# When SyncE announces expert weights, and where the residual rows are loaded, in a mixture-of-experts stage

## The chip, the cores and the metric

The kernel runs on one core of a Trainium2 chip. A core has engines that work side by side: TensorE (PE in the profile), VectorE (DVE), ScalarE (ACT), GpSimd (POOL) and SyncE (SP), which here only waits, counts and issues transfers. Sixteen DMA engines move data between HBM and the on-chip memory SBUF. The metric is the time of one launch on the device, in microseconds (us), as the median of several runs.

## The reference

One step of a hybrid decoder layer: modulated layer norm, a mixer (RG-LRU and Mamba-2 SSD), a residual with layer norm, then a hierarchical mixture of experts and a last residual with layer norm. The change is in the last two. Cut to what matters:

```python
def hmoe(v, ...):                      # v: 1032 rows (1024 prompt, 8 sample) of 1024
    # each row goes to 2 of 32 experts; rows are grouped by expert, 32 experts in all
    hb = jax.nn.silu(xb @ w_gate[e]) * (xb @ w_up[e])     # w_gate, w_up: 1024 x 512
    return hb @ w_down[e]                                  # w_down: 512 x 1024

f = hmoe(concat(vp, vs))
xp = layer_norm(alpha * xp + mp[:, 5] * f[:n_p], ln2_g, ln2_b)
xs = layer_norm(alpha * xs + ms[:, 5] * f[n_p:], ln2_g, ln2_b)
```

All is float32, so an expert has 2.1 MB each of gate, up and down weights, 6.3 MB together, and all 32 experts are read: 201 MB.

## The kernel before, in words

The first 900 us or so (mixer, first residual, routing) are not touched. The residual rows xp that the last layer norm needs are written to HBM (`xp1_d`) by then.

*Blocks.* The rows are sorted by expert and cut into blocks; this input gives 82. A block takes, on TensorE in this order: a turn of the previous block's hidden values (`h_turn`, line 2209), its own gate/up product (`gate_up`, line 2200, 64 matmuls), the turn of the input rows of the block after (`x_turn`, line 2188), and the down product of the previous block (`down`, line 2218, 32 matmuls). So the down product of block k comes behind the gate/up product of block k+1.

*Order of experts.* After three fixed ones the experts come in trios: a big one (3 to 9 blocks) and two small ones (1 or 2 blocks). Here x counts experts in this order, 0 to 31. The big ones are 3, 6, ... 27, growing; the small ones from expert 16 on have one block each. "Trio end" is the place where experts 1 or 2 after a big one and the next big one begin in three blocks in a row (19, 20, 21; 22, 23, 24; 25, 26, 27; 28, 29, 30).

*Weights.* They live in one large tile, `ring`. TensorE reads only the working copy `wcur`. Three slots (`GU_AT`) hold gate and up weights that have been fetched ahead, two (`DN_AT`) hold down weights. When a block belongs to a new expert, ScalarE copies the gate weights from slot to `wcur` (line 2000, four pieces of about 1 us) and VectorE the up weights (line 2579, four pieces of 0.7 us), each piece as soon as TensorE has used the matching quarter of the old ones (`gu_mm`). VectorE then copies the down weights (line 2592, one operation of 2.3 to 2.5 us) after the previous block's down product. On VectorE these stand between `h_out` of one block (lines 2541 and 2545, which makes the down product's input) and that of the next. On ScalarE the gate copy stands in front of `hb_out` (line 1972), which TensorE's next `h_turn` waits for.

*Announcements.* The copies don't wait for the loads themselves. SP waits for a load and then adds one to `gu_here` (gate and up) or `dn_here` (down); the copying engines wait for these counts:

```python
act.wait_ge(gu_here, here)
for q in range(QW):
    act.wait_ge(gu_mm, before * QW + (q + 1))
    act.activation(wcur[:, 1024 * q:1024 * q + 1024], ring[:, bass.ds(w + 1024 * q, 1024)], ...)
```

*SP's loop over experts.* SP does everything in one order. In iteration x it: waits for gate/up x and counts `gu_here`; waits until the down weights of x-1 have been copied and issues the load of down x+1 (line 1689); waits for down x and counts `dn_here`; waits until gate and up of x have been copied and issues the two loads of gate/up x+3 (line 1683). Where many transfers are queued an issue itself can take 4 to 6 us of SP's time. Behind the gate/up load in iteration 0 stand two tiles of residual rows (`xf[0]`, `xf[1]`, which have room of their own). In iteration 29 (`NE - 3`), where no gate/up load is left to do, stand six more tiles, the row `gate2` and the tile of eight sample rows; they go into gate/up slot `GU_AT[1]`. A tile is 128 rows of 1024, 0.52 MB.

*Other queues.* GpSimd gathers the input rows of each block (line 1833) and scatters its output rows (line 1841) by indirect DMA.

*The finale.* After the last scatter SP loads the result rows of each tile (`load_f`, line 1745, two loads of 0.52 MB per tile, four tiles ahead) into slot `GU_AT[2]`. For tile 0 ScalarE (line 2040) and VectorE (2641) combine them; for the others TensorE does (2254). VectorE then adds the residual tile `xf[t]` (2652) and does the layer norm's passes (2661, 2667). VectorE waits once for `gate2`, `ln2g`, `ln2b`.

Of the kernel before, what the change touches and what calls it, by code (L numbers as in the profile page):

```python
# [29 lines left out]
P = 128  # L30
D = 1024
KT = D // P
SEQ = 1024
NT = SEQ // P
DEC = 8
# [8 lines left out]
NE = 32  # L44
# [36 lines left out]
def build_step(nc, x_prompt, x_sample, c_prompt, c_sample, state_lru_conv, state_lru_h, state_ssd_conv,  # L81
# [13 lines left out]
    with ctx:  # L95
# [1531 lines left out]
        with nc.Block() as block:  # L1627
            @block.sync
            def _(sp):
# [72 lines left out]
                for x in (1, 2):  # L1702
                    load_gate_up(x, expert_at(x))
                    load_down(x, expert_at(x))
                for x in range(NE):
                    sp.wait_ge(gu_loaded[(x - 1) % 3 if x else 3], 32 * ((x + 2) // 3 if x else 1))
                    sp.sem_inc(gu_here, 1)  # L1707
                    if x >= 2 and x + 1 < NE:
                        e = expert_at(x + 1)
                        sp.wait_ge(down_copied, copied_down(x - 1))  # L1710
                        load_down(x + 1, e)
                    sp.wait_ge(dn_loaded[(x - 1) % 2 if x else 2], 16 * ((x + 1) // 2 if x else 1))
                    sp.sem_inc(dn_here, 1)
                    if x == 0:
                        sp.wait_ge(vector_once, IDXS_READY)
                        sp.wait_ge(tensor_once, TOKS_MM)
                        for b, n in ((0, 5), (1, 4)):
                            sp.wait_ge(xp1_stored[b], 16 * n)
                        load_gate_up(3, expert_at(3))
                        for t in range(2):  # L1720
                            sp.dma_start(xf[t], xp1_d[t * P:(t + 1) * P, :]).then_inc(xf_loaded[t], 16)
                    if x >= 1 and x + 3 < NE:
# [4 lines left out]
                        load_gate_up(x + 3, e)  # L1727
                    if x == NE - 3:
                        chunks = copied_gate_up(x)
                        sp.wait_ge(gate_copied, chunks)  # L1730
                        sp.wait_ge(up_copied, chunks)
                        for t in range(2, NT):
                            sp.dma_start(xf[t], xp1_d[t * P:(t + 1) * P, :]).then_inc(xf_loaded[t], 16)
                        sp.dma_start(gate2, mod_d[0:1, 5 * D:6 * D].to_broadcast([P, D])).then_inc(rows2n_loaded, 16)
                        sp.dma_start(xf[NT][0:DEC, :], xp1_d[SEQ:SEQ + DEC, :]).then_inc(xf_loaded[NT], 16)
                sp.wait_ge(down_copied, copied_down(NE - 2))
# [974 lines left out]
```

## Time and profile before

| | us |
|---|---|
| median of 3 runs | 1550.19 (1548.47 to 1551.68) |
| the profiled execution | 1546.65 |
| its span, first to last instruction | 1545.0 |
| TensorE busy | 1368.3 (89% of the span) |
| VectorE busy | 955.2 (62%) |
| ScalarE busy | 571.5 (37%) |
| first gate/up product of the expert stage | starts at 910.2 |
| last down product | starts at 1479.3 |

The profile is of one execution; times in it count from the span's start. The expert stage is some 570 us of it, the finale 63. A row of the timeline gives start and duration in us, engine, line, operation, and in brackets how long the engine stood idle before it and what ended that. "SPq" is SyncE's own instruction queue. DMA shares are of sixteen engines; 1.03 is what the rows show when they are all full.

### The profile page before, as it was taken

Reading aid. Unit: us, or ns where it says so; the run is one execution under the profiler, and the core shown is the slowest. Engines: PE = TensorE matmul, PEld = TensorE weight load, DVE = VectorE, ACT = ScalarE, POOL = GpSimd, SP = SyncE. Lnnn points to the kernel's source line nnn. Section 1 sums busy time; section 2 is a strip of 40 time slices with the busy share of each in tenths; the row PEclk is TensorE's granted clock in tenths of the full one; section 3 lists DMA queues with packets and bytes.
Section 4 is the critical chain, followed back from the end, with each engine's and each line's share of the span. In section 5 each row is a group of like instructions: output and inputs, shape, how many; then the busy total and the mean of one; then the engine's idle time right before and its main releaser. Section 6 shows DMA issues by size and latency. Waiting matters only on the chain.

```text
span 1545.0 us, 38250 instructions
## 1 busy us (share of the span) xinstructions
PE 1368.3 (89%) x13487; PEld 1010.1 (65%) x13487; DVE 955.2 (62%) x1702; ACT 571.5 (37%) x886; POOL 298.8 (19%) x325
## 2 busy tenths in 40 slices
PE   4799999999999998799999269899898999999864
PEld 3688989999888887687688145445454544545431
DVE  6655553968998889785775655444444244251549
ACT  3322322525556566621222014343334234141533
POOL 4000002210000000200000024333343333333320
PEclk9899999999999999899999579999999999999987
DMA  9666415644343345722225949999999897977763
GB/s 284 197 233 243 141 41 173 202 153 125 111 125 111 123 140 200 278 96 83 87 83 185 400 163 406 407 406 407 407 406 393 341 405 298 370 273 283 301 240 152
DMA packets 169586, 365.87 MB, mean 237 GB/s; under 512 B 16040, under 2 KB 94944, under 8 KB 166312
## 3 DMA queue, kind: packets, MB, share of 16 engines
q1 hardware_dynamic: 150616, 308.72, 54.5%
q0 software_dynamic: 18320, 54.08, 10.0%
q10 hardware_dynamic: 576, 2.10, 0.4%
q8 instruction: 45, 0.74, 0.2%
q14 instruction: 29, 0.24, 0.0%
HBM read 324.06 MB, written 45.63 MB: 239 GB/s over the span
## 4 chain that ended last, share of the span: by engine, by line
PE 38%; DVE 8%; DMA 5%; SPq 3%; issue 3%; ACT 1%; ACTq 1%; DVEq 0%; POOLq 0%
PE PS L2200 15%; PE PS L2069 10%; PE PS L2218 7%; DMA ring<-in_w_down_dram 5%; SPq L1683 2%; PE PS L2188 2%; PE PS L2209 2%; DVE ring L2592 1%; DVE big L2270 1%; PE PS L2100 1%; PE PS L2135 1%; DVE ring L2647 1%; PE PS L2092 1%; DVE ring L2652 1%; DVE ring L2661 1%
## 5 line engine op out<-in xcount | busy, mean ns | idle before, releaser
L939 PE MATMUL PS<-big 128*128 128x344 f32 x2592 | 426.0, 325 | 1.7 <-DVE big L1192 1.7
L939 PEld LDWEIGHTS PS<-big 128*128 128x128 f32 x2592 | 414.9, 191 | 10.4 <-issue 6.7
L2200 PE MATMUL PS<-ring,arena 128*32 128x256 f32 x5248 | 314.5, 394 | 0.5 <-DVE arena L2537 0.5
L2200 PEld LDWEIGHTS PS<-ring,arena 128*32 128x32 f32 x5248 | 167.5, 114 | 123.1 <-issue 29.8
L1833 POOL DMA_INDIRECT arena<-v_d,icur x84 | 103.4, 1231 | 315.0 <-DVE icur L2549 216.5
L2218 PE MATMUL PS<-ring,arena 128*32 128x256 f32 x2624 | 158.6, 382 | 1.0 <-DVE arena L2545 1.0
L2000 ACT ACTIVATE ring<-ring 128x1024 f32 x124 | 121.0, 1046 | 103.7 <-SPq L1707 84.1
L1841 POOL DMA_INDIRECT f_d<-arena,scur x82 | 107.9, 1316 | 55.6 <-issue 49.0
L2537 DVE COPY arena<-PS 128x256 f32<-128x256 f32 x82 | 34.7, 424 | 129.4 <-PE PS L2188 129.4
L2218 PEld LDWEIGHTS PS<-ring,arena 128*32 128x32 f32 x2624 | 77.1, 110 | 53.2 <-DVE arena L2545 1.3
L2541 DVE SCALAR_TENSOR_TENSOR arena<-arena,PS 128x128 f32<-128x128 f32 x82 | 23.6, 288 | 136.0 <-ACT arena L1977 99.8
L2579 DVE COPY ring<-ring 128x1024 f32 x124 | 80.3, 689 | 32.7 <-SPq L1707 26.1
L1972 ACT ACTIVATE arena<-PS 128x256 f32<-128x256 f32 x82 | 30.7, 374 | 179.7 <-PE PS L2200 179.7
L2069 PE MATMUL PS<-low 128*128 128x512 f32 x256 | 83.2, 407 | 11.0 <-ACTq L1913 5.1
L2592 DVE COPY ring<-ring 128x4096 f32 x31 | 74.7, 2409 | 28.9 <-PE PS L2218 28.9
L2069 PE MATMUL PS<-big,low 128*128 128x512 f32 x256 | 80.6, 397 | 0.0
L2069 PE MATMUL PS<-low,big 128*128 128x512 f32 x256 | 80.1, 395 | 0.0
L1982 ACT ACTIVATE arena<-PS 128x256 f32<-128x256 f32 x82 | 31.3, 382 | 116.1 <-PE PS L2218 116.1
L2209 PE MATMUL PS<-ident,arena 128*128 128x128 f32 x164 | 37.7, 314 | 40.3 <-ACT arena L1972 40.3
L2209 PEld LDWEIGHTS PS<-ident,arena 128*128 128x128 f32 x164 | 17.1, 146 | 74.4 <-ACT arena L1972 44.8
L2069 PEld LDWEIGHTS PS<-low 128*128 128x128 f32 x256 | 47.1, 193 | 21.8 <-issue 8.2
L1154 DVE TENSOR_TENSOR big<-arena,big 128x1024 fp32r<-128x1024 f32 x20 | 24.5, 1225 | 56.7 <-ACT big L713 56.6
(469 smaller groups left out, 1875.2 us busy)
## 6 DMA issues: line engine op xcount, KB each, us to landing
ring<-in_w_gate_dram SPq DMA_DIRECT2D x32, 2048.0 KB, 12.8
ring<-in_w_up_dram SPq DMA_DIRECT2D x32, 2048.0 KB, 18.7
ring<-in_w_down_dram SPq DMA_DIRECT2D x32, 2048.0 KB, 23.6
arena<-in_w_ada_dram SPq DMA_DIRECT2D x16, 1024.0 KB, 6.7
arena<-in_w_in_dram SPq DMA_DIRECT2D x20, 512.0 KB, 8.0
upper<-in_w_ada_dram SPq DMA_DIRECT2D x8, 1024.0 KB, 11.6
upper<-in_w_in_dram SPq DMA_DIRECT2D x16, 512.0 KB, 4.0
arena<-acs_d SPq DMA_DIRECT2D x8, 1024.0 KB, 4.7
```

Source lines behind the costliest of these rows:

```text
L939: mm = pe.matmul(PS[:, 3 * b + a, 0:CU], wss[b][:, i, k, :], us[:, j, k, a * CU:(a + 1) * CU], start=(k == 0 and (i, j) == PARTS[0]), stop ...
L1833: gp.indirect_dma_start(xg[b], None, v_q, bass.IndirectOffsetOnAxis(ap=icur[b][:, :], axis=0), bounds_check=QW * (SEQ + DEC) - 1, oob_is_e ...
L1841: gp.indirect_dma_start(f_q, bass.IndirectOffsetOnAxis(ap=scur[b][:, :], axis=0), yo[b], None, bounds_check=QW * 2 * (SEQ + DEC) - 1, oob_ ...
L1982: act.activation(yo[b], PS[:, 6, 0:DQ], ACT.Copy).then_inc(yo_ready, 1)
L2000: act.activation(wcur[:, 1024 * q:1024 * q + 1024], ring[:, bass.ds(w + 1024 * q, 1024)], ACT.Copy).then_inc(gate_copied, 1)
L2069: mm = pe.matmul(PS[:, bank + n, :], (yh[h % 2], yl3[h % 3])[a][:, k, :], (WH, WL)[b][i][:, 512 * n:512 * n + 512], start=(k == 0 and (a, ...
L2200: mm = pe.matmul(PS[32 * g:32 * g + 32, 3, 0:FH], xT[:, c, CAP * q:CAP * q + CAP], wcur[:, w:w + FH], start=(q == 0 and c == 0), stop=(q = ...
L2209: mm = pe.transpose(PS[:, 4, P * c:P * c + P], hb[:, P * c:P * c + P], ident[:, :])
L2218: mm = pe.matmul(PS[32 * g:32 * g + 32, 6, 0:DQ], hT[:, c % 2, CAP * (c // 2):CAP * (c // 2) + CAP], wcur[:, 8192 + 1024 * c + DQ * g:8192 ...
L2537: ve.tensor_copy(xT, PS[:, 0, 0:2 * P].rearrange("p (c t) -> p c t", c=2)).then_inc(xT_ready, 1)
L2579: ve.tensor_copy(wcur[:, 4096 + 1024 * q:5120 + 1024 * q], ring[:, bass.ds(w + (4096 + 1024 * q), 1024)]).then_inc(up_copied, 1)
L2592: ve.tensor_copy(wcur[:, GU:GU + DN], ring[:, bass.ds(w, DN)]).then_inc(down_copied, 1)
```

## The change

SP waits for gate/up x+1 and counts `gu_here` at the start of iteration x, where it did so at the start of iteration x+1; the count for expert 0 is made before the loop. The wait for down x and its count now stand before the load of down x+1. The two residual tiles of iteration 0 and the loads of iteration 29 are issued after the loop, behind all weights, together.

```diff
--- before.py
+++ after.py
@@ -1702,37 +1702,37 @@
                 for x in (1, 2):
                     load_gate_up(x, expert_at(x))
                     load_down(x, expert_at(x))
+                sp.wait_ge(gu_loaded[3], 32)
+                sp.sem_inc(gu_here, 1)
                 for x in range(NE):
-                    sp.wait_ge(gu_loaded[(x - 1) % 3 if x else 3], 32 * ((x + 2) // 3 if x else 1))
-                    sp.sem_inc(gu_here, 1)
+                    if x + 1 < NE:
+                        sp.wait_ge(gu_loaded[x % 3], 32 * ((x + 3) // 3))
+                        sp.sem_inc(gu_here, 1)
+                    sp.wait_ge(dn_loaded[(x - 1) % 2 if x else 2], 16 * ((x + 1) // 2 if x else 1))
+                    sp.sem_inc(dn_here, 1)
                     if x >= 2 and x + 1 < NE:
                         e = expert_at(x + 1)
                         sp.wait_ge(down_copied, copied_down(x - 1))
                         load_down(x + 1, e)
-                    sp.wait_ge(dn_loaded[(x - 1) % 2 if x else 2], 16 * ((x + 1) // 2 if x else 1))
-                    sp.sem_inc(dn_here, 1)
                     if x == 0:
                         sp.wait_ge(vector_once, IDXS_READY)
                         sp.wait_ge(tensor_once, TOKS_MM)
                         for b, n in ((0, 5), (1, 4)):
                             sp.wait_ge(xp1_stored[b], 16 * n)
                         load_gate_up(3, expert_at(3))
-                        for t in range(2):
-                            sp.dma_start(xf[t], xp1_d[t * P:(t + 1) * P, :]).then_inc(xf_loaded[t], 16)
                     if x >= 1 and x + 3 < NE:
                         e = expert_at(x + 3)
                         chunks = copied_gate_up(x)
                         sp.wait_ge(gate_copied, chunks)
                         sp.wait_ge(up_copied, chunks)
                         load_gate_up(x + 3, e)
-                    if x == NE - 3:
-                        chunks = copied_gate_up(x)
-                        sp.wait_ge(gate_copied, chunks)
-                        sp.wait_ge(up_copied, chunks)
-                        for t in range(2, NT):
-                            sp.dma_start(xf[t], xp1_d[t * P:(t + 1) * P, :]).then_inc(xf_loaded[t], 16)
-                        sp.dma_start(gate2, mod_d[0:1, 5 * D:6 * D].to_broadcast([P, D])).then_inc(rows2n_loaded, 16)
-                        sp.dma_start(xf[NT][0:DEC, :], xp1_d[SEQ:SEQ + DEC, :]).then_inc(xf_loaded[NT], 16)
+                chunks = copied_gate_up(NE - 3)
+                sp.wait_ge(gate_copied, chunks)
+                sp.wait_ge(up_copied, chunks)
+                for t in range(NT):
+                    sp.dma_start(xf[t], xp1_d[t * P:(t + 1) * P, :]).then_inc(xf_loaded[t], 16)
+                sp.dma_start(gate2, mod_d[0:1, 5 * D:6 * D].to_broadcast([P, D])).then_inc(rows2n_loaded, 16)
+                sp.dma_start(xf[NT][0:DEC, :], xp1_d[SEQ:SEQ + DEC, :]).then_inc(xf_loaded[NT], 16)
                 sp.wait_ge(down_copied, copied_down(NE - 2))
                 for dst, src in ((ln2g, ln2_g), (ln2b, ln2_b)):
                     sp.dma_start(dst, src.to_broadcast([P, D])).then_inc(rows2n_loaded, 16)
```

## Rows read from the trace of the kernel before

**Rows 1.** Table of waits, 910 to 1482 us, ScalarE, then TensorE (total, times, longest).

```profile
ACT ring L2000 <- SPq L1707: 84.1, 9, 38.9
...
PE PS L2209 <- ACT arena L1972: 40.3, 10, 7.3
```

**Rows 2.** Stretches: length, busy time and count by engine, TensorE's clock, DMA share, GB/s.

```profile
920.00:1170.00 250.00, 237.50 (x3688) 129.34 (x3684) 112.23 (x254) 89.06 (x166) 92.98 (x73) 0.97 1.03 407
1172.00:1180.00 8.00, 8.00 (x133) 4.34 (x126) 4.42 (x11) 6.56 (x10) 2.15 (x3) 1.00 0.86 331
1420.00:1440.00 20.00, 20.00 (x331) 11.04 (x324) 5.86 (x19) 7.41 (x14) 6.15 (x7) 1.00 0.12 39
```

**Rows 3.** Timeline at expert 27: start, duration, instruction [idle before, what ended it].

```profile
1363.81 3.66 PE L2200 MATMUL PS<-ring,arena 128*32 128x256 f32 x64
...
1370.07 3.66 PE L2200 MATMUL PS<-ring,arena 128*32 128x256 f32 x64
...
1375.65 3.90 ACT L2000 ACTIVATE ring<-ring 128x1024 f32 x4 [4.93 <-SPq L1707]
...
1379.87 0.69 PE L2209 MATMUL PS<-ident,arena 128*128 128x128 f32 x2 [3.83 <-ACT arena L1972]
...
1380.49 4.99 PE L2200 MATMUL PS<-ring,arena 128*32 128x256 f32 x64
```

**Rows 4.** Line 1689: down load of expert 26, ns and start, then landing.

```profile
L1689 SPq DMA_DIRECT2D ring<-in_w_down_dram x1: 4250/4250/4250, 1324.3 to 1324.3; - x1
...
DMA to landing us min/median/max: 25.0/25.0/25.0
```

**Rows 5.** Stretch after the stall of expert 27 (columns of rows 2).

```profile
1380.40:1382.00 1.60, 1.60 (x17) 0.80 (x20) 0.95 (x3) 0.28 (x1) 1.29 (x2) 0.50 1.02 417
```

**Rows 6.** Line 1689: down load of expert 18.

```profile
L1689 SPq DMA_DIRECT2D ring<-in_w_down_dram x1: 373/373/373, 1185.0 to 1185.0; - x1
...
DMA to landing us min/median/max: 13.3/13.3/13.3
```

**Rows 7.** Timeline of TensorE at expert 18.

```profile
1194.29 5.92 PE L2200 MATMUL PS<-ring,arena 128*32 128x256 f32 x64
...
1202.81 3.66 PE L2200 MATMUL PS<-ring,arena 128*32 128x256 f32 x64
...
1206.84 1.93 PE L2218 MATMUL PS<-ring,arena 128*32 128x256 f32 x32
```

**Rows 8.** Timeline of VectorE, ScalarE and TensorE at experts 28 to 30.

```profile
1440.26 0.29 DVE L2541 SCALAR_TENSOR_TENSOR arena<-arena,PS 128x128 f32<-128x128 f32 x1 [2.38 <-issue]
...
1444.42 3.66 PE L2200 MATMUL PS<-ring,arena 128*32 128x256 f32 x64
...
1446.97 0.29 DVE L2541 SCALAR_TENSOR_TENSOR arena<-arena,PS 128x128 f32<-128x128 f32 x1 [0.22 <-issue]
...
1453.49 3.90 ACT L2000 ACTIVATE ring<-ring 128x1024 f32 x4 [8.63 <-SPq L1707]
...
1457.71 0.69 PE L2209 MATMUL PS<-ident,arena 128*128 128x128 f32 x2 [7.33 <-ACT arena L1972]
```

**Rows 9.** Line 1689: down loads of experts 30 (lands first) and 31.

```profile
L1689 SPq DMA_DIRECT2D ring<-in_w_down_dram x2: 373/390/408, 1446.9 to 1458.9; - x2
...
DMA to landing us min/median/max: 10.2/11.7/13.3
```

**Rows 10.** Timeline of TensorE: the last two down products.

```profile
1475.99 1.91 PE L2218 MATMUL PS<-ring,arena 128*32 128x256 f32 x32
...
1479.30 1.93 PE L2218 MATMUL PS<-ring,arena 128*32 128x256 f32 x32 [1.03 <-DVE arena L2545]
```

**Rows 11.** Line 1738, issued at 1472.8: landing of two broadcast norm rows.

```profile
DMA to landing us min/median/max: 4.1/4.6/5.1
```

**Rows 12.** Chain that ended last, the finale's start (start, duration, what).

```profile
1484.74 0.33 SPq L1745
...
1485.11 4.53 DMA ring<-f_d
```


## The prediction, made before the changed kernel was run

> **What bounds the kernel now.** I read the waits first, then the stretches, then one stall in the timeline. TensorE is the serial line of the expert stage: 82 blocks, each a gate/up product, a turn and a down product. An undisturbed block takes 6.26 us (1370.07 - 1363.81) [rows 3]. The table of waits shows where it does not run: TensorE stood idle 40.3 us in ten waits for ScalarE's line 1972, and ScalarE stood idle 84.1 us in nine waits for SyncE's line 1707, the count `gu_here` [rows 1]. One of the nine (38.9 us) ends at the start of the stage, so 45.2 us are in eight. The stretches say what else is near: the DMA engines are full from 920 to 1170 us (407 GB/s), and before the last experts nearly idle (share 0.12) [rows 2]. So there are two regimes: up to about expert 18 the weights' traffic is a second limit just behind the queue's announcements, after it TensorE is alone.
>
> One stall, expert 27: TensorE's block begins at 1370.07. ScalarE copies the next expert's gate weights a quarter behind TensorE's quarters, so it could begin 3.66/4 = 0.9 us into the block and a little for the signal, at about 1371.2. It starts at 1375.65, when SP has issued another gate/up pair and only then counts `gu_here` up. ScalarE's `hb_out` is behind the copy, so TensorE's next turn is at 1379.87 after 3.83 us idle, and the block after it lasts 4.99 instead of 3.66 us [rows 3], at a granted clock of 0.50 [rows 5], the lower of the two levels (1.2 of 2.4 GHz), which it got after this idle time. The data was not late: the down load of expert 26 was issued after expert 27's gate/up and landed at 1324.3 + 25.0 = 1349.3 [rows 4]. Price: 1380.49 - 1370.07 - 6.26 = 4.16, plus 4.99 - 3.66 = 1.33, together 5.5 us. Two more trios (experts 21 and 24) have the same stall at 3.8 us idle each; expert 30's is 7.33 us idle, since seven residual loads and a broadcast row are issued in front of its announcement [rows 8].
>
> **Part 1, announcing a step sooner.** In iteration x SP now waits for gate/up x+1 and counts before it waits for anything that compute releases. Expert 27 would be announced before 1349.3, 22 us ahead of need. This adds no instruction; it makes `load_down(x+1)` wait behind two landings, gate/up x+1 and down x. The first of these was queued before down x, so it adds nothing to the second. At the landing of down x the queue still holds gate/up x+2, 4.19 MB or 10.3 us at 407 GB/s [rows 2]. SP answers a landing in 0.7 us (1472.16 to 1472.8), and a 0.52 MB row then lands in 4.1 us of which 1.3 are transfer, so 2.8 us of latency [rows 11]: 3.5 us against 10.3 of cover. Without that cover each expert would cost the difference; that is the slower rival.
>
> What is late next? A stall that goes is replaced by the next limit, the landing of the down weights. From a down landing to the down product takes 1475.99 - 1472.16 = 3.83 us (VectorE's copy 2.3 to 2.5, then `h_out`, which stands behind it on VectorE) [rows 9, 10].
>
> *Experts 1 to 18.* Here several stalls would vanish one after another (about 30 us in blocks 0 to 41 by the same reckoning), but the transfers don't get faster, so I take the last limit. Expert 18's down weights landed at 1185.0 + 13.3 = 1198.3 [rows 6], its down product began at 1206.84 [rows 7]: slack 8.5 - 3.83 = 4.7 us. The full queue itself moves earlier by the two residual tiles that are no longer in it, 1.05 MB / 407 = 2.6 us, and perhaps by the 1.4 us that a dip in it cost (1172 to 1180: share 0.86 where 1.03 is full) [rows 2]. So 7.3 to 8.7 us, I take 8.0. TensorE then waits at that place (the removed stalls exceed the limit) and restarts at the low level: 1.33 us at expert 27, 5.92 - 3.66 = 2.26 at expert 18 [rows 3, 7]; I take 1.6. Term: 6.4, bounds 5.0 (7.3 - 2.3) and 8.7 (no restart).
>
> *Trios 21, 24, 27.* 3 x 5.4 = 16.2 us can go. Is the down load in time? In the last trio, for which the same positions hold, down 30 was issued by an event that doesn't move in its block's frame and landed at 1446.9 + 10.2 = 1457.1 [rows 9]. With no stall the blocks after the one at 1444.42 [rows 8] start at 1450.68 and 1456.94, and the down product 4.03 us later (1206.84 - 1202.81) [rows 7], at 1460.97. Needed: 1457.1 + 3.83 = 1460.9. It fits with nothing to spare. VectorE is the other limit: a round with both copies takes 1446.97 - 1440.26 = 6.71 us [rows 8], 0.45 over TensorE's 6.26; two such rounds put the third `h_out` at 1460.4 and, after its two operations of 0.29, its result at 1461.0, or 1461.4 with copies of 2.5. I take 0.5 us lost per trio, bounds 0 and 0.9. Term: 14.7, bounds 13.5 and 16.2.
>
> **Part 2, residual tiles last.** *Before the finale*, in the frame of the trace: expert 30 isn't held at 1453.5 any more, and down 31 is not behind 3.7 MB. It is issued when down 30 has landed (1457.2; expert 29's copy is done before 1446.97 + 6.71 = 1453.7), alone in the queue: 2.8 + 2.10 MB / 407 = 8.0 us, landed 1465.2, down product of block 80 at 1469.0 (unheld it would be about 1467), last down product 3.3 later (1479.30 - 1475.99 [rows 10]) at 1472.3 instead of 1479.3: 7.0 us earlier, and the first result load could be issued at 1484.74 - 7.0 = 1477.7 [rows 12].
>
> *The finale.* Nine residual tiles, the gate row and two norm rows are 8 x 0.524 + 3 x 0.524 + small = 5.83 MB, 14.3 us. They start at 1465.2 + 0.7 + 2.8 = 1468.7 and end at 1483.0; the result rows `f12` are behind them on SP's queue. Tile 0 (1.05 MB) is there at 1485.6, against 1485.11 + 4.53 = 1489.64 [rows 12]: 4.0 us earlier, not 7.0. SP's issuing (some ten issues of 0.4 us) is hidden in this. Tiles 1 and up come every 2.6 us while VectorE takes 5.2 a tile, so nothing else moves. Term: 4.0. Bounds: 7.0 if these loads overlap freely, 1.3 if the last scatter also has to wait for the queue to drain.
>
> The Trainium skill, page "DMA: Bandwidth & Descriptors", section "Queues, rings and completion order", says that each DMA engine takes turns between the queue rows it has work for, a packet at a time. By it GpSimd's last scatter is slowed but doesn't stand behind SP's loads, which gives the 4.0; strict order would give 1.3. No row here separates the two. The same page, section "Where 436 GB/s comes from", says that about 358 GB/s of HBM bind such loads; the row of 920 to 1170 us shows 407, so the measurement decides. By 358 the finale would be 16.3 instead of 14.3 us and the sum 2 us worse.
>
> **Sum.** 6.4 + 14.7 + 4.0 = 25.1 us, bounds 19.8 and 31.9. The profiled execution took 1546.65 us (span 1545.0 and 1.65 around it), which gives 1521.5; it is 3.5 under the median of the three runs, so for the median of 1550.19 I say 1525.1, bounds 1530.4 and 1518.3.
>
> **Rivals.**
>
> *Down weights take the place of the announcement.* The fit above has no margin: if in three consecutive rounds of copies, gathers and scatters down x lands 2 us later, each of the four last trios keeps 2 us and a restart of 1.6, 14.4 in all: a gain of 10.7, 1539.5 us. For it: the zero margin. Against it: the queue is otherwise idle there [rows 2], and nothing is added to it.
>
> *All of it is real.* No restart at expert 18, no VectorE loss, finale uncontended: 31.9 us, 1518.3. Against it: the finale's bytes are certain.
>
> *No change.* SP's count isn't what holds the copy. Rows 3 and 4 speak against it (data 26 us old when the copy starts). 1550.
>
> *Slower: the queue runs dry.* The change lets fewer transfers stand in the queue at each down landing (4.19 instead of 6.29 MB). If DMA engines ran dry for b us at each of the 15 experts 4 to 18, the cost is 15b; it eats the whole gain at b = 1.7 and at 2.5 gives 1562 us. For it: the dip at 1172 to 1180, while a down load was still pending. Against it: it is one dip of 1.4 us in 250, and 10.3 us of cover against 3.5.
>
> The page's section "Rules for kernel authors" tells to issue a DMA early and wait for it late, and the moved residual tiles do the opposite. As a mechanism here this is the finale's contention. Priced from rows it takes 3.0 of the 7.0 us and can't turn the sign alone: without the gain ahead of it, down 31 (issued at 1458.9 into an empty queue, landed 1466.9) would have its followers through at 1484.7, when the result loads are only issued.
>
> **Chances.** Forecast 0.67; down weights late 0.12; all real 0.08; something larger 0.03; no change 0.04; slower 0.06. The range 1515 to 1539 holds the forecast, the full gain and half of the second. A difference within 0.2% (3 us) is about what a measurement of this kernel can't tell from none. Faster 0.90, same 0.04, slower 0.06.
>
> **What would show it.** Right: ScalarE's copy no longer waits for SyncE's count; TensorE's ten waits shrink to a few at the landings of down weights before expert 19; blocks at 6.26 us through experts 19 to 30; the DMA share stays at 1.03 from 920 on. In the finale one packed stretch of DMA ahead of the result rows, ScalarE waiting for them. Wrong: dips in the DMA share after each down landing, VectorE or SP named at each expert change, or the result rows landing as late as before.

## The result, and the profile after

The changed kernel took 1527.31 us, median of 4 runs (1522.45 to 1529.17), where the kernel before took 1549.34 in the same comparison: ratio 0.9851, 95% interval 0.9825 to 0.9876. The prediction was 1525.1, in the range 1515 to 1539. A second comparison of the same two kernels gave 0.9875 (0.9855 to 0.9895). The profiled execution took 1527.24 us, its span is 1525.3.

The table of waits, 910 to 1482 us, of the kernel after; the rows answer to [rows 1]:

```profile
ACT ring L2000 <- PE PS L2200: 58.0, 30, 36.6
...
DVE ring L2592 <- SPq L1712: 41.3, 10, 7.4
...
PE PS L2218 <- DVE arena L2545: 21.9, 7, 5.0
...
PE PS L2209 <- ACT arena L1972: 1.4, 1, 1.4
...
ACT ring L2000 <- SPq L1710: 0.8, 1, 0.8
```

ScalarE waits for SyncE's `gu_here` once for 0.8 us, where it was 84.1 us in nine waits. Of these 84.1, the 38.9 us at the start of the stage have not gone: the wait there is 36.6 us now and is put down to TensorE (line 2200). What went is the 45.2 us of the other eight. TensorE's waits for `hb_out` fell from 40.3 to 1.4 us. In their place stand waits for the down weights: VectorE 41.3 us for `dn_here` (line 1712), TensorE 21.9 us at down products for `h_out`.

The stretches of the kernel after (columns as in [rows 2]):

```profile
920.00:1170.00 250.00, 237.50 (x3712) 128.43 (x3706) 112.50 (x257) 90.96 (x169) 92.38 (x74) 0.97 1.03 406
1172.00:1180.00 8.00, 8.00 (x132) 4.25 (x124) 5.08 (x14) 5.80 (x10) 2.04 (x2) 1.00 0.96 372
1400.00:1420.00 20.00, 20.00 (x322) 10.86 (x318) 5.86 (x19) 7.26 (x15) 6.17 (x7) 1.00 0.25 97
```

The DMA engines are as full as before up to 1170 us, and the dip at 1172 to 1180 is most of the way closed (share 0.96 for 0.86). Before the last experts they are still mostly idle (0.25 in the third row).

*Where the time went.* The kernel's first part, which the change doesn't touch, ended at 910.23 us in one profile and at 911.81 in the other. So I compare places in the expert stage from each kernel's own first gate/up block, and give each as a difference. A block's excess is its length over the undisturbed 6.26 us.

| us from the stage's first block | before | after | earlier by |
|---|---|---|---|
| down product of expert 18 | 296.61 | 289.80 | 6.8 |
| block 45, after expert 18 | 311.36 | 307.27 | 4.1 |
| block 77, before the last trio end | 527.93 | 507.65 | 20.3 |
| last down product | 569.06 | 543.02 | 26.0 |
| ScalarE begins tile 0 of the result | 579.43 | 558.02 | 21.4 |
| end of the span | 634.80 | 613.53 | 21.3 |

The expert stage alone is 26.0 us shorter and the finale gives 4.8 back. The excess of all blocks fell from 55.2 us in 19 blocks to 25.6 in six; the six are at big experts 6, 9, 12 and 18 (4.3, 6.5, 6.8 + 0.5, 7.0 + 0.8 us). The trio ends of experts 21 to 30, which lost 5.3 us and more each, are free.

The timeline of the kernel after at expert 27, which answers to [rows 3]:

```profile
1358.03 3.90 ACT L2000 ACTIVATE ring<-ring 128x1024 f32 x4 [0.57 <-PE PS L2200]
...
1363.06 3.66 PE L2200 MATMUL PS<-ring,arena 128*32 128x256 f32 x64
...
1369.32 3.66 PE L2200 MATMUL PS<-ring,arena 128*32 128x256 f32 x64
...
1369.81 2.29 DVE L2592 COPY ring<-ring 128x4096 f32 x1 [1.96 <-SPq L1712]
...
1373.41 1.93 PE L2218 MATMUL PS<-ring,arena 128*32 128x256 f32 x32
```

ScalarE's copy is ended by TensorE's quarter, not by SyncE; the blocks follow at 6.26 us. The last two rows are the prediction's narrow fit: VectorE waits 1.96 us for the down weights of expert 27, copies them, and the down product begins 4.09 us behind the gate/up product in front of it, where 4.03 is undisturbed. There was no margin.

At expert 18, answering to [rows 7]:

```profile
1192.51 3.66 PE L2200 MATMUL PS<-ring,arena 128*32 128x256 f32 x64
...
1198.43 2.29 DVE L2592 COPY ring<-ring 128x4096 f32 x1 [7.38 <-SPq L1712]
...
1201.62 3.64 PE L2218 MATMUL PS<-ring,arena 128*32 128x256 f32 x32 [5.01 <-DVE arena L2545]
1205.19 0.69 PE L2209 MATMUL PS<-ident,arena 128*128 128x128 f32 x2
1205.81 4.41 PE L2200 MATMUL PS<-ring,arena 128*32 128x256 f32 x64
```

Here the down weights are the limit: their load is in the chain that ended last, up to its landing at 1198.26.

```profile
1182.56 15.70 DMA ring<-in_w_down_dram
```

TensorE stands 5.01 us and then works at the low level of its clock, as the stretch behind the wait shows (its granted clock is the 0.50):

```profile
1201.60:1204.00 2.40, 2.38 (x24) 1.19 (x28) 0.55 (x3) 0.00 (x0) 0.72 (x1) 0.50 1.03 410
```

The finale of the kernel after, in the chain that ended last (compare [rows 12]):

```profile
1428.24 10.42 DMA ring<-in_w_down_dram
...
1440.00 7.99 DMA ring<-in_w_down_dram
...
1451.50 1.93 PE PS L2218 x32
...
1454.83 1.98 PE PS L2218 x32
...
1458.10 6.29 DMA f_d<-arena,scur
...
1464.45 0.34 SPq L1745
...
1465.78 6.58 DMA ring<-f_d
```

The first two rows are the loads of the down weights of experts 30 and 31. The last scatter took 6.29 us. In the kernel before, where SyncE's norm rows had landed by then [rows 11], the same row of the chain reads:

```profile
1482.56 2.11 DMA f_d<-arena,scur
```

The result rows of this chain, the fourth load of line 1745, took 6.58 us; they are not those of [rows 12] (4.53), which belong to the second load, so these two are not compared. What stood in SyncE's queue meanwhile, by its timeline:

```profile
1448.70 0.82 SPq L1733 DMA_DIRECT2D arena<-xp_d  x2
1449.57 3.14 SPq L1733 DMA_DIRECT2D ring<-xp_d  x6
1452.75 0.50 SPq L1734 DMA_DIRECT2D ring<-mod_d  x1
1453.30 0.38 SPq L1735 DMA_DIRECT2D ring<-xp_d  x1
1454.50 0.36 SPq L1738 DMA_DIRECT2D ring<-in_ln_g_dram  x1
1454.90 1.26 SPq L1738 DMA_DIRECT2D ring<-in_ln_b_dram  x1
```

The two norm rows of line 1738 landed 10.6 and 12.4 us after their issue, the later one at 1467.3.

### The profile page after: what moved, and what is told of

Its sections match the earlier page's. It is cut to its first block, busy times and chain, and to the rows that moved or that the text cites. A ratio compares the mean times of both kernels' runs of the same rounds, so it can differ in the third digit from the quotient of the medians.

```text
span 1525.3 us, 38250 instructions
## 1 busy us (share of the span) xinstructions
PE 1360.6 (89%) x13487; PEld 1005.5 (66%) x13487; DVE 952.6 (62%) x1702; ACT 572.0 (37%) x886; POOL 295.9 (19%) x325
## 3 DMA queue, kind: packets, MB, share of 16 engines
q1 hardware_dynamic: 150616, 308.72, 55.2%
## 4 chain that ended last, share of the span: by engine, by line
PE 29%; DMA 19%; DVE 7%; issue 2%; SPq 1%; ACT 0%; DVEq 0%; POOLq 0%; ACTq 0%
DMA ring<-in_w_down_dram 18%; PE PS L2069 10%; PE PS L2200 8%; PE PS L2218 5%; DVE big L2270 1%; PE PS L2188 1%; PE PS L2100 1%; DMA ring<-in_w_up_dram 1%; PE PS L2135 1%; PE PS L2209 1%; DVE ring L2647 1%; DVE ring L2652 1%; PE PS L2092 1%; DVE ring L2661 1%; SPq L1678 1%
## 5 line engine op out<-in xcount | busy, mean ns | idle before, releaser
L939 PEld LDWEIGHTS PS<-big 128*128 128x128 f32 x2592 | 411.9, 189 | 10.4 <-issue 6.7
L2200 PE MATMUL PS<-ring,arena 128*32 128x256 f32 x5248 | 301.0, 381 | 0.5 <-DVE arena L2537 0.5
L2200 PEld LDWEIGHTS PS<-ring,arena 128*32 128x32 f32 x5248 | 162.1, 110 | 114.2 <-issue 15.0
L2218 PE MATMUL PS<-ring,arena 128*32 128x256 f32 x2624 | 165.1, 394 | 21.9 <-DVE arena L2545 21.9
L2218 PEld LDWEIGHTS PS<-ring,arena 128*32 128x32 f32 x2624 | 78.7, 112 | 78.4 <-DVE arena L2545 23.7
L2592 DVE COPY ring<-ring 128x4096 f32 x31 | 72.7, 2345 | 55.9 <-SPq L1712 41.3
L2069 PEld LDWEIGHTS PS<-low,big 128*128 128x128 f32 x256 | 49.3, 193 | 10.9
L2069 PEld LDWEIGHTS PS<-big,low 128*128 128x128 f32 x256 | 49.2, 192 | 10.8
```

The source lines that it names most:

```text
L939: mm = pe.matmul(PS[:, 3 * b + a, 0:CU], wss[b][:, i, k, :], us[:, j, k, a * CU:(a + 1) * CU], start=(k == 0 and (i, j) == PARTS[0]), stop ...
L2069: mm = pe.matmul(PS[:, bank + n, :], (yh[h % 2], yl3[h % 3])[a][:, k, :], (WH, WL)[b][i][:, 512 * n:512 * n + 512], start=(k == 0 and (a, ...
L2200: mm = pe.matmul(PS[32 * g:32 * g + 32, 3, 0:FH], xT[:, c, CAP * q:CAP * q + CAP], wcur[:, w:w + FH], start=(q == 0 and c == 0), stop=(q = ...
L2218: mm = pe.matmul(PS[32 * g:32 * g + 32, 6, 0:DQ], hT[:, c % 2, CAP * (c // 2):CAP * (c // 2) + CAP], wcur[:, 8192 + 1024 * c + DQ * g:8192 ...
L2592: ve.tensor_copy(wcur[:, GU:GU + DN], ring[:, bass.ds(w, DN)]).then_inc(down_copied, 1)
```

## Experiments

Diffs are against the changed kernel unless said otherwise. Ratios are to the kernel before, with 95% intervals. "In the frame" means counted from the stage's first block, as in the table above.

### The changed kernel again

> The changed kernel once more, to compare the next ones with it on one chip: 1527 us, ratio 0.985 to the kernel before.

1527.34 us, ratio 0.9875 (0.9855 to 0.9895). In the frame every place lies within 0.4 us of the first profile and the end within 0.02 us, so the column "after" does not depend on one execution. The kernel before has one profile only.

### The announcements alone

The residual loads go back to iterations 0 and 29:

```diff
                         load_gate_up(3, expert_at(3))
+                        for t in range(2):
+                            sp.dma_start(xf[t], ...)
...
+                    if x == NE - 3:
+                        (waits for the copies; tiles 2 to 7, gate2, sample rows)
-                (the same behind the loop, with tiles 0 to 7)
```

> Part 1 alone: announcements a step sooner and the down load behind the wait for the down weights, with the residual tiles back in their old places. Theory (announcements remove the stalls, the weights' traffic caps experts 4 to 18, the finale's traffic takes some back): the trios of experts 21, 24, 27 stay free of stalls as in the changed kernel. The two early tiles (1.05 MB, 2.6 us at 407 GB/s) are back in the full queue, so the down product of expert 18 comes 2 to 3 us later than with the whole change. At the end down 31 is again behind 3.7 MB (9 us), so the last down product is about 5 us later than in the changed kernel (1454.8), but the results' loads find an almost empty queue and the scatter takes 2.1 instead of 6.3 us, which gives about the same back. Sum: 2 to 4 us slower than the changed kernel, about 1530 us, 19 us faster than before. Rival (moving the residual tiles is itself the larger part): 1540 or more.

1530.94 us, ratio 0.9883 (0.9868 to 0.9898); in the frame 16.1 us shorter than before. Expert 18's down product is 3.8 us earlier than before (6.8 with both parts). Its down weights land at 289.5 in the frame, which is 1.5 us later than in the kernel before (288.1) and 3.1 later than with both parts (286.4):

```profile
1183.64 16.00 DMA ring<-in_w_down_dram
```

Blocks 45 to 77 take 200.5 us, as with both parts (200.4), where the kernel before took 216.6: the gain at the trio ends is the announcements' alone. What the second part changes is seen in the tail, in the chain that ended last:

```profile
1440.47 14.09 DMA ring<-in_w_down_dram
...
1466.60 2.10 DMA f_d<-arena,scur
```

The last down load, queued behind what is left of 3.7 MB of residual tiles and gate row, takes 14.09 us instead of 7.99, and TensorE's wait at that down product is 8.39 us (3.34 with both parts). The last down product comes 10.2 us later than with both parts, twice the 5 us expected. In exchange the last scatter takes 2.10, and the finale as a whole is 5.1 us shorter, so the sum came out near the forecast all the same.

### The residual tiles alone

The old loop, and all residual loads behind it:

```diff
                 for x in range(NE):
-                    if x + 1 < NE:
-                        (wait for gate/up x+1, count gu_here)
-                    (wait for down x, count dn_here)
+                    (wait for gate/up x, count gu_here)
                     (load_down(x + 1))
+                    (wait for down x, count dn_here)
```

> Part 2 alone: all nine residual tiles behind the last weights, announcements as before. Theory: the stalls at experts 6 to 27 stay as they were (3.8 to 5.3 us idle each); expert 30's shrinks from 7.3 to about 3.8 us idle because nothing is issued in front of its announcement; of these 3.8 us gained some 1 is lost to the finale's traffic. About 3 us faster than before, 1546. Rival (the finale's traffic costs more than that stall, so part 2 alone is slower): 1551 or more.

1543.0 us, ratio 0.9958 (0.994 to 0.9976); 4.8 us shorter in the frame, of which 2.8 are there at block 45. ScalarE still waits for `gu_here` (84.3 us in 11 waits), and TensorE for ScalarE:

```profile
ACT ring L1997 <- SPq L1707: 84.3, 11, 37.7
...
PE PS L2206 <- ACT arena L1969: 36.8, 10, 5.7
```

The excess of blocks 48, 57 and 67 is 4.1 us each as before, that of 78 to 80 together 6.7 for 9.3. The two parts gave 16.1 and 4.8 alone and 21.3 together: they add up to within 0.4 us. The rival "no change" is out, since moving the counts alone took ScalarE's waits and 16.1 us away.

### Half the down weights of experts 5 to 18

```diff
-                    sp.dma_start(ring[:, w:w + DN]..., w_down[0, bass.ds(e, 1)]...)
+                    c = FF // P // 2 if 5 <= x <= 18 else FF // P
+                    sp.dma_start(ring[:, w:w + 1024 * c]..., w_down[0, bass.ds(e, 1), 0:c * P]...)
```

> The changed kernel, but the down loads of experts 5 to 18 bring only half of their rows (1.05 instead of 2.10 MB); the other half of the slot keeps older weights, so this leaves out part of the loading. Theory (the weights' traffic is the limit there): a sixth less traffic is 12.9 us per expert against 14.6 of TensorE work, so the waits at the down products of experts 6, 9, 12 and 18 (together 25 us over undisturbed blocks) go, and the profile's span is 22 to 26 us shorter, about 1500 to 1503, with VectorE's rounds at changes of expert the next limit at 0 to 0.5 us each. Rival (those waits come from SP's order of waiting, or from VectorE's rounds of copies): the waits stay, 1520 or more.

This kernel leaves out half of what these loads bring. One run: 1504.85 us. The sum of the excess is -0.1 us, so no block up to expert 18 is held any more, and block 45 begins 26.0 us sooner than with full loads, as much as their whole excess of 25.6. This shows the limit that is left: at the four big experts among the first 19 the weights arrive too late. The edit removes more traffic (14.7 MB) than the waits needed, so it gives no price per us of transfer.

### The down load in front of the wait for the landing

```diff
-                    sp.wait_ge(dn_loaded[...], ...)
-                    sp.sem_inc(dn_here, 1)
                     if x >= 2 and x + 1 < NE:
                         sp.wait_ge(down_copied, copied_down(x - 1))
                         load_down(x + 1, e)
+                    sp.wait_ge(dn_loaded[...], ...)
+                    sp.sem_inc(dn_here, 1)
```

> The whole change, but load_down(x+1) is issued before the wait for down x again, as in the kernel before. It asks what that move costs. Theory (10 us of cover make it free at experts 4 to 18; it costs only at the end, where down 31 is issued when down 30 has landed, 1440.0, although expert 29's copy was done at 1434.3): the waits at the down products of experts 6, 9, 12, 18 stay within 0.5 us of the changed kernel's (4.3, 6.5, 6.8, 7.8 us over an undisturbed block, restart included); down 31 is issued about 5 us sooner, the 3.3 us wait at the last but one down product goes, the residual tiles are through 4 to 5 us sooner, and the whole is 4 to 6 us faster than the changed kernel, about 1522. Rival (the queue runs short at each down landing in the changed kernel): the early waits shrink by 1 us or more each, and the time is 1517 or less.

1524.58 us, ratio 0.9839 (0.9821 to 0.9857). The intervals overlap with the changed kernel's, so the gain is read in the frame: 2.5 us, where 4 to 6 were expected. The early blocks keep 4.8, 6.5, 6.8 and 6.0 us (sum 25.1 for 25.6), and expert 18's down product is no sooner (290.2 in the frame for 289.8): the queue hadn't run dry behind the landings, so the slower rival has nothing here. Block 42 alone went from 7.0 + 0.8 to 6.0, more than the 0.5 us allowed for. What it does change is the tail. The last down load goes out at 1433.97 instead of 1440.00, its down product is not held any more, and the last one is 4.1 us sooner in the frame; the end is only 2.5 sooner, since the scatter again runs beside the residual loads (the chain of this kernel) and is issued 4.1 us after the last down product, where it was 3.3:

```profile
1454.95 5.91 DMA f_d<-arena,scur
...
1460.92 0.34 SPq L1745
```

### Eight more tiles in the finale

To see how the last scatter and the result rows share the DMA engines with what SyncE has queued, 4.19 MB of further loads are issued behind the residual tiles, into a slot that is free:

```diff
+                (waits for the copies of the last expert)
+                for t in range(NT):
+                    sp.dma_start(ring[:, GU_AT[0] + D * t:GU_AT[0] + D * (t + 1)], xp1_d[t * P:(t + 1) * P, :])...
```

> The changed kernel with eight more loads of residual tiles (4.19 MB, 10.3 us) into a slot that is free, behind the eight real ones: the finale's suspected cost almost doubled. Theory: the first result tile is there 10 us later and the span is 10 us longer, 1535. It also tells how the last scatter shares the DMA engines: if the queues take turns, it lands some 6 us after its issue as in the changed kernel and the result loads are issued at about 1464 to 1466; if it stands behind SyncE's queue, it lands 10 us later and they are issued at about 1475, and the span is 13 us longer. Rival (the finale isn't held by this traffic): span unchanged.

One run: 1532.89 us, 8.4 longer in the frame than the changed kernel, where 10 were expected. Its chain:

```profile
1455.80 5.48 DMA f_d<-arena,scur
1461.30 0.02 SPq L1755
1461.35 0.33 SPq L1751
...
1463.10 15.47 DMA ring<-f_d
```

The scatter, on GpSimd's queue, takes 5.48 us, no longer than with half the bytes ahead of it (6.29). The result rows, on SyncE's own queue, take 15.47 instead of 6.58, 8.9 more, against 10.3 us of added transfer. So a full queue of SyncE's delays this scatter by a few us that did not grow when the queue did, and delays SyncE's own later loads by most of what was added. By the rule of the Trainium skill, page "DMA: Bandwidth & Descriptors", section "Queues, rings and completion order" (the engines take turns between queue rows, a packet at a time), that is what one would see. The two scatters agree with it and rule out a strict order, in which the scatter would have stood behind all eight added tiles, all issued before it, by 1455.0.

### Half of the residual tiles behind the first result rows

On top of the experiment with the down load in front: tiles 4 to 7 and the sample rows are issued behind the result rows of the first four tiles.

```diff
-                for t in range(NT):
+                for t in range(RING):
                     sp.dma_start(xf[t], ...)
...
+                (behind the result rows of the first four tiles)
+                for t in range(RING, NT):
+                    sp.dma_start(xf[t], ...)
```

> As the kernel with the down load issued before the down wait (1524.6), and residual tiles 4 to 8 are loaded behind the first eight result loads instead of in front of them. Theory (what stands in front of the result rows in the full queue, and slows the last scatter, is the finale's price): 9.1 instead of 14.3 us of traffic end at about 1456 in that kernel's frame, the last scatter lands 3 us after its issue instead of 6, the first tile is there 3 us sooner, the time is 1521 to 1522. Rival (the scatter's 6 us are its own, or tiles 4 to 8 come late for VectorE's passes, 5.2 us a tile): no gain, 1524 or more.

1519.91 us, ratio 0.9829 (0.9809 to 0.9849), the shortest time of a kernel that loads everything; 6.1 us shorter in the frame than the changed kernel. The scatter's row in the chain is now

```profile
1454.12 4.10 DMA f_d<-arena,scur
```

and tile 0's first pass begins 12.8 us after the last down product, where it was 15.0 in the changed kernel and 10.4 in the kernel before. The chain shows something that the changed kernel has not, a scatter of an earlier block, issued together with the residual loads:

```profile
1444.64 8.13 DMA f_d<-arena,scur
```

ScalarE waits 1.3 us for its landing before it can write the last block's output, and so the last scatter is issued later. With the down load in front the same wait is 1.8 us. An earlier start of the residual loads moves them onto this scatter.

### Two of the tiles back among the weights

On top of the last: tiles 0 and 1 are issued in iteration 24, where the queue is idle.

```diff
+                    if x == NE - 8:
+                        for t in range(2):
+                            sp.dma_start(xf[t], ...)
```

> As the kernel with the split, and residual tiles 0 and 1, which have room of their own, are loaded in iteration 24, behind gate/up 27, where the DMA engines have idle time (1330 to 1350). Theory: 6.5 us of traffic are left in front of the finale and end before the last scatter is issued; it lands after 2.1 us as in the kernel before, the result loads are issued at once, and the first tile is there 1 to 1.5 us sooner than with the split: 1520. The trio at experts 25 to 27 stays free of stalls. Rival (these loads delay down 26 or 27 and the stall comes back): 1524 or more.

1522.21 us, ratio 0.9837 (0.9816 to 0.9857). The last scatter takes 2.11 us, as alone (the earlier one still 8.12, and ScalarE waits 1.4 us for it), and the frame is 1.0 us shorter than the last one's; the intervals of the two ratios overlap, so the medians don't tell them apart (this execution's untouched first part was 2.9 us longer).

### Gate and up behind the big expert's down load

The limit that is left is the down weights of big experts, which stand in the queue behind gate/up pairs that are needed later. Here the pairs 7, 10, ... 28 are issued behind that down load. The edits from here on are on top of the split of the residual tiles.

```diff
+                HELD = range(4, 26, 3)
...
                         load_down(x + 1, e)
+                    if x - 1 in HELD:
+                        (waits for the copies of x-1)
+                        load_gate_up(x + 2, e)
...
-                    if x >= 1 and x + 3 < NE:
+                    if x >= 1 and x + 3 < NE and x not in HELD:
```

> As the split kernel (1519.9), and the gate/up load that follows the small experts before a big one (gate/up 7, 10, 13, 16, 19, 22, 25, 28) is issued behind the big expert's down load instead of in front of it. The waits that are left (experts 6, 9, 12, 18, 25.6 us in all) end at the landing of a big expert's down weights, behind 4.19 MB that aren't needed for three blocks or more. Theory (limit is the traffic in front of those down weights): they need 10.3 us less in front of them, a saving that counts once over the stage because the traffic itself stays, with one or two restarts less; the waits shrink from 25.6 to some 12 to 15 us and the time to 1507 to 1510. Rival (the queue is too short at the landings now: a down load of 5.2 us of traffic covers SP's 3.5 us, and the DMA engines run dry): the waits stay above 20 us and the time above 1515.

Missed: 1575.04 us, ratio 1.0148 (1.013 to 1.0165), slower than the kernel before. The table of waits of this kernel:

```profile
DVE ring L2601 <- SPq L1723: 67.8, 7, 13.3
...
PE PS L2227 <- DVE arena L2554: 53.2, 7, 11.3
```

and SyncE's own:

```profile
SPq L1711 <- DMA ring<-in_w_up_dram: 193.5, 25, 11.4
```

(84.4 us in 24 waits in the changed kernel.) TensorE's waits at down products grew from 21.9 to 53.2 us: at blocks 42, 50, 59 and 69 the excess is 12 to 13 us each, where the changed kernel lost 7.0 at the first and nothing at the others. SyncE waits in the changed loop for gate/up x+1 before down x. With the pair now issued behind down x, that wait ends last, and the down weights are announced only when the pair behind them has landed. The chain shows it at expert 18, from the pair's load to the count:

```profile
1184.18 17.86 DMA ring<-in_w_up_dram
...
1203.82 0.02 SPq L1723
```

I had moved the transfers and overlooked the announcements. The rival of the expectation, an emptier queue, is there too: the DMA share is 0.20 from 1176 to 1184 us and 0.80 from 1170 to 1200, where the changed kernel has 1.01. What that part costs wasn't separated.

### The same, with the residual loads moved as well

Further: tiles 0 and 1 in iteration 24, and tiles 2, 3 and the gate row issued before the wait for the last down load.

> The same, with residual tiles 0 and 1 in iteration 24, and the residual tiles 2 and 3 with the gate row issued before the wait for down 31 instead of behind it. Theory: what stands in front of the first result rows starts 3.5 us sooner (SP's answer and a transfer's latency) and is 1.05 MB less; it is through before the last scatter is issued, which lands in about 2 us; 2 us faster than the kernel before it, about 1506. Rival (the finale is no longer held by this traffic): equal.

Missed with it: 1571.43 us, ratio 1.0114 (1.0096 to 1.0133). In the frame it ends within 0.2 us of the one before, so the residual loads' place gains nothing here.

### The swap, with the announcement of down x first

In the iterations in which the pair stands behind down x, SyncE now waits for and counts down x before it waits for gate/up x+1:

```diff
-                    if x + 1 < NE:
+                    if x + 1 < NE and x - 2 not in HELD:
                         (wait for gate/up x+1, count gu_here)
...
                     (wait for down x, count dn_here)
+                    if x - 2 in HELD:
+                        (wait for gate/up x+1, count gu_here)
```

> The swap of loads was 25 us slower than before instead of 10 us faster than the split kernel. Its trace shows waits of 12 to 13 us at the down products of experts 18, 21, 24 and 27, ended by SyncE's count for the down weights, while SyncE itself waited for gate/up x+1, which the swap had put behind down x. Here, in the iterations of big experts, SyncE waits for down x and counts it before it waits for gate/up x+1. Theory (it was only the order of SyncE's two waits): those waits go, the gain of the swap appears, waits of 12 to 15 us in all and 1507 to 1511 us. Rival (the loads themselves come too late in that order, the queue runs dry): 1520 or more.

Missed again: 1548.22 us, ratio 0.9966 (0.9949 to 0.9983). In the frame it is 27.3 us better than the swap alone, which had lost 51.2 us to the split kernel: the order of the two waits was about half of that loss. The excess at blocks 42, 50, 59 and 69 is still 7.4, 7.0, 7.6 and 7.8 us. The other blocks have 20 us more, mostly in steps of about 1 us; the sum is 50.2 us, 25.9 in the split kernel, and these steps are not explained here. For the four blocks the chain that ended last shows the reason, at expert 18:

```profile
1186.70 5.33 SPq L1683
...
1193.65 4.64 SPq L1689
1198.29 0.06 issue
1198.35 0.02 SPq L1723
...
1198.49 0.09 DVE ring L2604
```

The last wait is not for data. SyncE spends 5.33 us in the issue of the pair's second half and 4.64 in the issue of the down load of expert 19, both into a full queue, and counts `dn_here` for expert 18 right behind, at 1198.35. VectorE had waited 7.97 us for that count. The load of down 18 had been issued at 1181.71 into a queue that was nearly empty (the DMA share was 0.23 from 1180 to 1182 and 0.48 from 1182 to 1184), so it probably landed near 1190, an estimate by the 7.99 us of the last down load; its landing isn't in the records, and this last step is argued. The queue ran low here too (share 0.89 from 1180 to 1200), which this experiment doesn't separate. One of the two issues, the down load of expert 19, stands in front of the count because the split kernel has the load in front of the wait for the landing.

### The same, with the residual loads moved

> The same correction on the kernel with the residual tiles 0 and 1 in iteration 24 and the others in front of the wait for down 31. Theory: 2 us faster than the one before it, 1505 to 1509. Rival: equal to it, since the finale isn't held any more.

1545.2 us, ratio 0.9947 (0.9927 to 0.9968): missed as well, with the same excess at the four blocks (7.4, 7.1, 7.6 and 7.7 us), and in the frame within 0.3 us of the one before. Whether the swapped order of transfers would pay if the counts didn't stand behind long issues stays open. Neither the changed kernel's order with the swap (count down x, then issue) nor an announcement from another queue was tried.

## Why the prediction was right, and where its terms were off

The mechanism was right: SyncE's serial order held the copies, not the data, and with the count moved the down weights were the next limit. The medians of one comparison lie 22.0 us apart. The forecast for the profiled execution was 25.1 us; in the frame it was 21.3 (1.6 of them given back in that execution by its longer first part). By terms:

| term | predicted (bounds) | measured |
|---|---|---|
| experts 1 to 18 | 6.4 (5.0 to 8.7) | 4.1 |
| trio ends 21, 24, 27 | 14.7 (13.5 to 16.2) | 16.2 |
| to the last down product | 7.0 | 5.7 |
| given back in the finale | 3.0 (0 to 5.7) | 4.8 |
| sum | 25.1 (19.8 to 31.9) | 21.3 |

The sum is inside its bounds partly by luck. The first term is below its lower bound of 5.0, and what the rows of the tail leave together ("to the last down product" less "given back"), predicted as 4.0 with bounds 1.3 and 7.0, is 0.9, below as well. The term between came out at its upper bound.

**Experts 1 to 18.** The limit was named rightly, the down weights of expert 18, but its down product came 6.8 us earlier, not 8.0 (below the bound of 7.3): 3.8 by the announcements and 3.1 by the two tiles, for 4.7 and 2.6. The slack of 4.7 us was there, and from the landing to the product it took 3.36 us instead of 3.83. But the landing moved up only 1.6 us (288.1 [rows 6] to 286.4 in the frame), not 2.6 to 4.0. The prediction let the landings stay where they were when only the counts move; with the counts alone this one came 1.5 us later than before, and the 3.1 us of the tiles came off from there. Why it came later no run shows. And the restart cost 2.7 us instead of 1.6: the down product 3.64 for 1.93, the turn 0.69 for 0.44, the gate/up 4.41 for 3.66. The prediction had priced the gate/up product alone, by [rows 3] and [rows 7]; here the idle time fell in front of a down product, and three instructions in a row ran below full clock. That is outside its bound of 2.3.

**Trio ends.** All of the 16.2 us. I had taken off 0.5 per trio for VectorE; it took nothing, since VectorE stood idle for 1.96 us before the copy of the down weights, and these came in time, to within 0.07 us at block 69. The rival "down weights take the place of the announcement" would have needed them 2 us later.

**To the last down product.** The load lasted 7.99 us, as predicted (8.0), and its product came 11.5 us after the issue (11.8). The step that failed is "it is issued when down 30 has landed": the chain shows down 30's landing at 1438.66 and the issue at 1440.00. SyncE first counted and then read two values from memory, the expert's number and the count to wait for (`expert_at` and `copied_down`), 1.34 us that stand behind the landing because the wait was moved in front of the load. This is nearly all of the missing 1.3 us, and the experiment that puts the load in front gets it back and more.

**The finale.** The bytes were right: the loads were predicted to be through at 14.3 us plus 3.5 after the landing of the last down load, which is 1465.8 in the trace after, and the last norm row landed at 1467.3. But the cost was put in the wrong place. I let the result rows stand behind the loads and gave the scatter nothing. In fact the scatter took 4.2 us longer (6.29 for 2.11), and the result rows, issued at 1464.45 when the loads were nearly through, only about 0.5 more before ScalarE could begin (5.38 us after the first issue for 4.92). The prediction used the rule of turns (the Trainium skill, page "DMA: Bandwidth & Descriptors", section "Queues, rings and completion order") for "not behind the loads". It also said from it that the scatter is slowed, and left that without a price. A strict order, for which the prediction had kept the term at 1.3, would have made the scatter grow with the queue, and with 4.19 MB more it didn't.

**The slower rival.** The DMA share stayed at 1.03 from 920 to 1170 us, and the load issued ahead of the landing changed nothing there. The queue did not run dry there.

## What to carry to other kernels

When one queue waits, counts and issues in one order, read for each consumer what ends its wait: the data's landing, or an unrelated wait or a blocking issue in front of the count. Announce in the order in which the data lands. The load of a free slot in front of the wait for a landing won 2.5 us here where the queue was short, but into a full queue its issue held the next count up by 4.64 us. A large load moved to the very end can cost twice: it slows the stores beside it, and it delays whatever is queued behind it; issue only as much of it there as the next steps need.

## What the runs showed of the hardware

- The last GpSimd scatter beside a full SyncE queue took 5.5 to 6.3 us from issue to landing, 2.1 alone and 4.1 with a few tiles in the queue. Doubling the bytes queued did not lengthen it. A scatter issued together with the residual loads took 8.1.
- After 5.01 us of idle time TensorE had the low clock (0.50) for a down product of 3.64 us for 1.93 and lost 2.7 us before it ran at full speed again. In the kernel before, 3.8 us of idle time cost 1.3 [rows 3].
- Issuing a 2.1 MB load into a full queue held SyncE 4.6 to 5.3 us in the rows above, where it takes 0.37 into an empty one; everything behind it in program order, counts too, came that much later.
